# Order of work in a two-layer decoder trunk on 8 cores: row stores ahead of a routing chain, a weight load ahead of index scatters, norms one tile ahead, subtractions on another engine

## The chip, the cores and the metric

The kernel runs on all 8 cores of one Trainium2 chip. Each core takes one batch element of 2048 tokens and computes it alone; the cores exchange nothing. Cores 0 to 3 stand on one die, cores 4 to 7 on the other. The metric is the device time of the slowest core, in microseconds (us), lower is better.

The engines of a core are called PE (TensorE), DVE (VectorE), ACT (ScalarE), POOL (GpSimd) and SP (SyncE). Each runs its own instructions in program order and waits for the others by semaphores. SP, ACT and POOL issue DMAs.

## The reference

Two layers, and in each a token mixer, a hierarchical mixture of experts, and a gated embedding of the layer:

```
for i in range(2):
    xn = rms_norm(h, g_mix[i])
    mix = conformer_conv(xn) if i == 0 else moba_attention(xn)
    h = h + mix
    h = h + hier_moe(rms_norm(h, g_ffn[i]))        # group top-1, expert top-2 of 16
    h = h + sigmoid(rms_norm(h, g_ple[i]) @ w_gate) * (p[i] @ w_proj)

conformer_conv: u = xn @ w_pw1 + b; a, g = split(u); u = a * sigmoid(g)
                u = causal depthwise conv of width 31, over positions
                u = silu(layer_norm(u)) @ w_pw2 + b
hier_moe:       a group by softmax over 4, then 2 of its 4 experts, weights renormalised
                expert e: (silu(x @ w_gate[e]) * (x @ w_up[e])) @ w_down[e]
```

The model width is 1024, the expert hidden width 512, and a token goes to 2 of 16 experts.

## The kernel before

The residual stream h stays on chip, features on the partitions: 8 chunks of 128 features by 2048 tokens in float32. Tokens are worked in four tiles (tt 0 to 3) of 512. A small scheduler (`Sched`) puts a semaphore wait ahead of each instruction for every region that it reads or overwrites. The order of the instructions on each engine is the order in which the program's functions are called, so an engine that waits holds back all that was emitted behind it. DMAs of SP and ACT take their completion semaphores in turn from one pool, those of POOL from another (L60). A DMA waits for the last use of its semaphore.

The phases run in this order: A (convolution mixer), B0 (experts of layer 0), C0 (combination and embedding), D (attention), B1, C1.

**Phase A** (L578). At the start x is loaded in 16 DMAs, four for each tile. `rms_tile` (L557) makes a norm: ScalarE squares the eight chunks into two alternating buffers `sq`, TensorE sums them by a matmul with ones, ScalarE takes logarithm and exponential to give `rstd`, VectorE writes the normalised chunks `xgA`. `pw1(c, tt)` (L627) takes two groups of 8 matmuls, a sigmoid on ScalarE into one of two `sg` buffers chosen by tt, and a product on VectorE into `gp`. For each tile the norm and `pw1` of c = 0 and 1 are called; then `pw1` of the other chunks alternates with the convolution of chunk c - 2. `regroup` stores `gp` and reads it back in another layout. When the sums of the layer norm are complete, a loop over 32 groups (L695) subtracts the mean (`t1A`, on VectorE or POOL), multiplies by `rstd` (`t2A`, VectorE) and applies silu (ScalarE). After every four groups a store goes to memory and four loads bring it back as `xgA`, two of them issued by ScalarE, which waits for the store. `pw2(tt)` (L709) is the last matmul of the phase. It is not called there but handed to phase B as `tile_fn`. In layer 1 attention hands over its output projection in the same way.

**Front of phase B** (L954 to L1039), once for each layer. `front(tt)` (L833) squares and sums a tile and makes the router's logits, in turns between ScalarE and TensorE. `xnorm(tt)` writes the normalised tile `xnb`, `rows(tt)` (L824) transposes it into four blocks of 128 tokens, copies each on ScalarE into one of three `xrow` buffers, and stores it to memory in rows (`xnd`) by SP. `back(t0, nt)` (L850) is the routing chain of nt blocks of 128 tokens: some 90 small VectorE instructions, a prefix sum on TensorE (`Mall`), two products on POOL, and at its end two indirect DMAs per block from POOL, which scatter token numbers of 4 bytes into a list in memory (`idxd`). `wts` (L930) makes the combination weights: small VectorE instructions, one exponential on ScalarE, three POOL instructions that read `r_A`. `back` of the last four blocks writes `r_A` anew.

`load_w(e)` (L736) loads the weights of expert e into one of three ring buffers, in three DMAs. In layer 0 POOL issues them, with a cast from float32; in layer 1 SP issues them, from bfloat16 copies made during attention. The third ring buffer lies over memory of the mixer (its last weights and inputs), so `load_w(2)` waits for the last matmul of `tile_fn(3)`.

**The experts** then run one after the other: three gathers of 128 rows each from `xnd`, transposes, gate and up matmuls, silu and product, the down matmuls, and stores. Weights of expert e + 3 are loaded when expert e is done.

Of the kernel before, what the change touches and what calls it, by code (L numbers as in the profile page):

```python
# [18 lines left out]
NTT = 4  # L19
# [23 lines left out]
class Sched:  # L43
    def __init__(self, nc, ctx):
        self.nc = nc
        self.ctx = ctx
        self.eng = {'pe': nc.tensor, 'act': nc.scalar, 'dve': nc.vector, 'pool': nc.gpsimd, 'sp': nc.sync}
        self.sem = {}
        self.cnt = {}
        self.nsem = 0  # L50
        for e in ['pe', 'act', 'dve', 'pool']:
            self._new_sem(e)
        self.seen = {e: {} for e in self.eng}
        self.W = {}
        self.R = {}
        self.pend = {e: [] for e in self.eng}
        self.dma_sems = []
        self.dma_cnt = []
        self.dma_rr = {'hw': 0, 'sw': 0}
        self.dma_pool = {'hw': list(range(0, 8)), 'sw': list(range(8, 32))}  # L60
        for i in range(32):
            self.dma_sems.append(ctx.enter_context(nc.semaphore(f"dq{i}")))
            self.dma_cnt.append(0)
        self.nwaits = 0
        self.nops = 0
        self.addr = {}
        self.holes = [(SB0, SB1)]
        self.nm = 0
# [371 lines left out]
def build_program(phases=('A', 'B0', 'C0', 'D', 'B1', 'C1'), debug=False):  # L440
# [28 lines left out]
    with ExitStack() as ctx:  # L469
# [34 lines left out]
        def xn(c, lo, n):  # L504
            return xg[0][:, c, lo:lo + n]
# [51 lines left out]
        def rms_tile(tt, gname, gl, out_fn):  # L557
            ps = next_ps()
            for c in range(NC8):
                S.act(sq[:, c % 2, :], h[:, c, tts(tt)], AF.Square)  # L560
                S.mm(ps[:], ones_bf[:], sq[:, c % 2, :], start=(c == 0), stop=(c == NC8 - 1))
            S.act(rt[:], ps[:], AF.Ln, bias=EPS, scale=1.0 / D)
            S.act(rstd[:], rt[:], AF.Exp, scale=-0.5)
            for c in range(NC8):
                S.stt(out_fn(c), h[:, c, tts(tt)], P(gname, gl * 8 + c), rstd[:], ALU.mult, ALU.mult)
# [12 lines left out]
        def phase_A(pc):  # L578
# [3 lines left out]
            if True:  # L582
# [68 lines left out]
                def conv(c):  # L651
                    for gg in range(4):
# [7 lines left out]
                        if g:  # L660
                            stats(g - 1)

                for tt in range(NTT):
                    rms_tile(tt, 'g_mix', 0, lambda k, t1=tt: xn(k, t1 * TT, TT))
                    for c in range(2):
                        pw1(c, tt)
                S.copy('dve', blk[:], cva[:, NG * 36:NG * 36 + 128])
# [26 lines left out]
                ps_set[0] = list(range(8))  # L694
                for g in range(NG):  # L695
                    v = gc[:, g, 8:GW]
                    S.tt('dve' if g % 5 in (1, 3) else 'pool', t1[:, g % 3, :], v, mean[:], ALU.subtract)
                    S.tt('dve', t2[:, g % 3, :], t1[:, g % 3, :], rstd[:], ALU.mult)
                    S.act(v, t2[:, g % 3, :], AF.Silu, bias=P('ln_bP', g), scale=P('ln_gP', g))
                    c, gg = g // 4, g % 4  # L700
                    if gg == 3:
                        S.dma('sp', gpd[c], gc[:, 4 * c:4 * c + 4, 8:GW], outs=[("gpd", 0, 1, c, c + 1)])
                        for q in range(4):
                            S.dma('sp' if q % 2 else 'act', xg[0][32 * q:32 * q + 32, c, :].rearrange("p (i u) -> p i u", i=4),
                                  gpd[c].rearrange("(i c) g u -> g c i u", c=32)[q], ins=[("gpd", 0, 1, c, c + 1)])
# [14 lines left out]
        def phase_B(l, tile_fn, prev):  # L720
            EC = CO['ecol']
            with ExitStack() as pc:
# [97 lines left out]
                def xnorm(tt):  # L820
                    for c in range(NC8):
                        S.stt(xnb[:, tt % 2, c, :], h[:, c, tts(tt)], P('g_ffn', l * 8 + c), rstd[:], ALU.mult, ALU.mult)

                def rows(tt):  # L824
                    for i4 in range(4):
                        i = tt * 4 + i4
                        pb = next_ps()[:].bitcast(BF16)
                        for c in range(NC8):
                            S.transpose(pb[:, c * 128:(c + 1) * 128], xnb[:, tt % 2, c, i4 * 128:(i4 + 1) * 128], idb[:])
                        S.copy('act', xrow[:, i % 3, :], pb)  # L830
                        S.dma('sp', xnd[i * 128:(i + 1) * 128, :], xrow[:, i % 3, :], outs=[("xnd", 0, 1, i, i + 1)])
# [18 lines left out]
                def back(t0, nt):  # L850
# [71 lines left out]
                    S.tt('dve', ri[:], ri[:], ok2[:], ALU.mult)  # L922
                    S.ts('dve', ri[:], ri[:], dumpi[:], ALU.add, 0.0, ALU.max)
                    S.ts('dve', isl[:, T1], ri[:], float(NIDX - 1), ALU.min)
                    for i in range(t0, t0 + nt):
                        for k in range(2):
                            S.dma('pool', idxd, tokid[:, i:i + 1], out_idx=isl[:, i, k:k + 1],
                                  ins=[("idx", 0, 1, 50, 51)], outs=[("idx", 0, 1, 2 * i + k, 2 * i + k + 1)])
# [40 lines left out]
                front(2)  # L969
                rows(1)  # L970
                xnorm(2)
                back(0, 12)
                wts(0, 12)
                tile_fn(3)
                prev.close()
                ring.append(sb(f"ring_{l}_2", [128, 3 * NIN], BF16, pc))
                load_w(2)
                rows(2)
                front(3)
                back(12, 4)  # L980
                xnorm(3)
                rows(3)
                S.dma('sp', xi[:], idxd[0:IX1, :].rearrange("(p a) o -> p (a o)", p=128), ins=[("idx", 0, 1, 0, 51)])
# [761 lines left out]
```

How the kernel before makes its waits and increments, by code:

```python
    def _wait(self, engine, toks):  # L179
        need = {}
        for (sem, val, src) in toks:
            k = id(sem)
            if k not in need or need[k][1] < val:
                need[k] = (sem, val, src)
        for k, (sem, val, src) in need.items():
            if src == engine and engine == 'pe':
                continue
            if self.seen[engine].get(k, 0) < val:
                self.eng[engine].wait_ge(sem, val)
                self.seen[engine][k] = val
                self.nwaits += 1
# [19 lines left out]
    def op(self, engine, fn, ins=(), outs=(), inc=True):  # L211
# [6 lines left out]
                self._new_sem(engine)  # L218
            self.cnt[engine] += 1
            ins_obj.then_inc(self.sem[engine], 1)
            tok = (self.sem[engine], self.cnt[engine], engine)
# [907 lines left out]
        def overflow(l, nov_i, tok_nov, ovf, ring, xt, xT_, hdn, ysb, idb2, wfull, xs, c_loads, some):  # L1129
# [53 lines left out]
                for hc in range(4):  # L1183
                    A_.activation(out=sil[:, hc, :], in_=PS[hc][:, 0:n], func=AF.Silu)
                to(V)
                for hc in range(4):
                    V.tensor_tensor(out=hd[:, hc, :], in0=PS[4 + hc][:, 0:n], in1=sil[:, hc, :], op=ALU.mult)
            with nc.If(some > 0):
                for e in engs_:
                    for sem, cnt in state:
                        if cnt:
                            e.wait_ge(sem, cnt)
                nc.all_engine_barrier()
                nov, deep = val(1, NOV), val(2, 1)
                with nc.If(nov > NSP):
```

## Time and profile before

| | us |
|---|---|
| median of three runs | 2541.95 |
| lowest and highest | 2538.1 to 2543.45 |
| the profiled execution | 2535.46 |
| its span, core 5, the slowest | 2534.4 |
| its fastest core, core 1 | 2450.0 |

| engine of core 5 | busy us | share |
|---|---|---|
| PE matmul | 1796.5 | 71% |
| DVE | 941.1 | 37% |
| ACT | 836.5 | 33% |
| POOL | 462.2 | 18% |

The chain that ended last is PE for 48%, DMA 23%, DVE 10%, issue 7%, ACT 6%, another core or an unknown queue 4%. Times in all rows are us from the start of the core's span, and of core 5 if no other core is named. "Another core or an unknown queue" and "remote" stand for a release that the profile can't attribute. Names such as `ps<-xgA,w` are output and inputs of an instruction, `x32` is how many are merged in the row, and the bracket at a row's end says how long the engine was idle ahead of it and what ended that.

### The profile page before, as it was taken

What the parts mean: (1) busy time and instruction counts of PE and PEld (TensorE: products, weight loads), DVE (VectorE), ACT (ScalarE), POOL (GpSimd) and SP (SyncE); (2) the same over time, 40 slices, a digit from 0 to 9 for tenths busy, and PEclk for the clock granted to TensorE, in tenths of its full rate; (3) what the DMA queues carried; (4) which work ended last, traced back from release to release, by engine and by line L of the source; (5) the groups of instructions that cost most, each with busy time, mean ns of one, the idle gap of its engine ahead of it and who ended that gap; (6) DMA issues with size and microseconds to landing.
All of it is one profiled execution on the core that took longest, in us unless ns stands there. A gap on an engine that the chain in (4) does not pass through costs nothing.

```text
span 2534.4 us, 34160 instructions; the slowest of 8 cores (2450.0 to 2534.4 us)
## 1 busy us (share of the span) xinstructions
PE 1796.5 (71%) x11032; PEld 989.0 (39%) x11032; DVE 941.1 (37%) x1720; ACT 836.5 (33%) x1330; POOL 462.2 (18%) x522
## 2 busy tenths in 40 slices
PE   4799358329766666477777888787884269998587
PEld 1244122115333333233255666555622135554333
DVE  2566543332211111266533333333233223232265
ACT  2333413112111111156445555555421212222253
POOL 0000310422111111243200000000003121112354
PEclk8799678669887777678899999989987679999688
DMA  7153444148999999741276666696842059999862
GB/s 186 39 171 111 104 102 81 45 78 157 199 205 188 183 178 183 187 145 50 35 105 87 89 93 102 98 109 96 124 126 67 32 135 308 284 290 301 232 188 96
DMA packets 100593, 354.10 MB, mean 140 GB/s; under 512 B 13344, under 2 KB 25632, under 8 KB 81968
## 3 DMA queue, kind: packets, MB, share of 16 engines
q0 software_dynamic: 45472, 197.78, 45.5%
q1 hardware_dynamic: 52080, 150.79, 18.1%
q10 hardware_dynamic: 2848, 3.15, 0.5%
q8 instruction: 98, 1.61, 0.3%
q14 instruction: 95, 0.78, 0.1%
HBM read 393.61 MB, written 137.95 MB: 210 GB/s over the span
## 4 chain that ended last, share of the span: by engine, by line
PE 48%; DMA 23%; DVE 10%; issue 7%; ACT 6%; another core or an unknown queue 4%; POOL 1%; ACTq 0%; DVEq 0%; SPq 0%; POOLq 0%
PE ps L261 45%; DMA xt<-xnd,xi 12%; DMA ysd<-ysb 5%; PE ps L265 3%; DMA xt<-xnd,xs 2%; DMA gb<-ysd,slots 1%; ACT pt L278 1%; DMA gpd<-gc 1%; ACT sq L278 1%; DMA h<-xP 1%; DVE q L299 1%; DVE xgC L299 1%; DMA ring<-w 1%; DVE xnb L299 1%
## 5 line engine op out<-in xcount | busy, mean ns | idle before, releaser
L261 PE MATMUL ps<-xTT,ring 128*128 128x384 bf16 (+1 forms) x2304 | 367.6, 321 | 38.6 <-DVE ysb L305 22.9
L261 PEld LDWEIGHTS ps<-xTT,ring 128*128 128x128 bf16 x2304 | 218.2, 100 | 187.3 <-issue 58.1
L261 PE MATMUL ps<-xgA,w 128*128 128x512 bf16 x768 | 193.7, 408 | 86.4 <-DMA xgA<-gpd 69.0
L278 ACT ACTIVATE pt<-ps,cst_s 128x512 bf16<-128x512 f32 (+1 forms) x288 | 181.0, 658 | 83.2 <-PE ps L261 76.4
L261 PE MATMUL ps<-xgD,wh 128*128 128x512 bf16 x512 | 144.8, 434 | 85.7 <-DVE q L299 56.7
L265 PE MATMUL ps<-idb,xt 128*128 128x128 bf16 x800 | 72.2, 256 | 187.4 <-DMA xt<-xnd,xi 162.5
L261 PE MATMUL ps<-ring,hdn 128*128 128x512 bf16 x800 | 204.1, 416 | 0.3 <-DVE hdn L281 0.3
L261 PE MATMUL ps<-sq,ones_bf 128*128 128x512 bf16 x256 | 104.1, 443 | 113.5 <-ACT sq L278 110.2
L261 PE MATMUL ps<-xgC,ring 128*128 128x512 bf16 x512 | 144.0, 420 | 25.9 <-DVE h L281 14.3
L278 ACT ACTIVATE sq<-h 128x512 bf16<-128x512 f32 x192 | 111.0, 623 | 152.1 <-PE ps L261 124.7
L281 DVE TENSOR_TENSOR hdn<-ps,sgs 128x384 bf16<-128x384 f32 (+1 forms) x144 | 75.0, 527 | 229.8 <-PE ps L261 193.4
L261 PEld LDWEIGHTS ps<-xgA,w 128*128 128x128 bf16 x768 | 77.8, 102 | 200.4 <-issue 123.2
L304 ACT COPY ysb<-ps 128x512 f32<-128x512 f32 x100 | 57.9, 586 | 294.7 <-PE ps L261 198.5
L261 PE MATMUL ps<-qT,kT 128*128 128x256 bf16 x576 | 145.9, 278 | 0.5 <-ACT pt L278 0.4
L305 DVE COPY ysb<-ps 128x512 f32<-128x512 f32 x100 | 69.1, 692 | 199.6 <-PE ps L261 105.0
L261 PE MATMUL ps<-rh,esl 72*128 72x256 bf16 x576 | 142.9, 278 | 0.0
L265 PEld LDWEIGHTS ps<-idb,xt 128*128 128x128 bf16 x800 | 60.3, 115 | 201.3 <-issue 198.8
L244 POOL DMA_INDIRECT xt<-xnd,xi x96 | 92.9, 968 | 216.1 <-PE ps L265 187.4
L261 PEld LDWEIGHTS ps<-ring,hdn 128*128 128x128 bf16 x800 | 83.4, 106 | 105.1 <-issue 33.9
L278 ACT ACTIVATE sgs<-ps 128x384 f32<-128x384 f32 (+1 forms) x144 | 66.1, 468 | 175.3 <-PE ps L261 173.0
L305 DVE COPY xTT<-ps 128x1024 bf16<-128x1024 bf16 x68 | 46.9, 689 | 202.0 <-PE ps L265 172.8
L261 PE MATMUL ps<-vh,pt 128*128 128x129 bf16 x1088 | 113.6, 227 | 7.9 <-DVE pt L281 5.7
(209 smaller groups left out, 2631.1 us busy)
## 6 DMA issues: line engine op xcount, KB each, us to landing
ring<-w_moe POOLq DMA_DIRECT2D x48, 1024.0 KB
ysd<-ysb SPq DMA_DIRECT2D x96, 512.0 KB
w<-w_moe POOLq DMA_DIRECT2D x48, 1024.0 KB
ring<-w SPq DMA_DIRECT2D x48, 1024.0 KB
ysd<-zt SPq DMA_DIRECT2D x19, 512.0 KB
xnd<-xrow SPq DMA_DIRECT2D x32, 256.0 KB
yT<-h SPq DMA_DIRECT2D x32, 256.0 KB
h<-xP SPq DMA_DIRECT2D x14, 512.0 KB
```

What stands on the lines that cost most here:

```text
L244: ins_obj = self.eng[queue].indirect_dma_start(out, bass.IndirectOffsetOnAxis(out_idx, 0) if out_idx is not None else None, in_, bass.Indi ...
L261: return self.op('pe', lambda e: e.matmul(out, lhsT=lhsT, rhs=rhs, start=start, stop=stop, **kw), ins=[lhsT, rhs], outs=[out], inc=inc)
L265: return self.op('pe', lambda e: e.transpose(out, in_, ident), ins=[in_, ident], outs=[out])
L278: return self.op('act', lambda e: e.activation(out=out, in_=in_, func=func, **kw), ins=ins, outs=[out])
L281: return self.op(eng, lambda e: e.tensor_tensor(out=out, in0=in0, in1=in1, op=op), ins=[in0, in1], outs=[out])
L299: return self.op('dve', lambda e: e.scalar_tensor_tensor(out=out, in0=in0, scalar=scalar, in1=in1, op0=op0, op1=op1), ins=ins, outs=[out])
L304: return self.op('act', lambda e: e.copy(out=out, in_=in_), ins=[in_], outs=[out])
L305: return self.op(eng, lambda e: e.tensor_copy(out=out, in_=in_), ins=[in_], outs=[out])
```

## The change

It does these things:

- The semaphores for DMAs of SP and ACT become 12 instead of 8, those of POOL 20 instead of 24.
- In phase A the norm of tile tt + 1 is emitted ahead of `pw1` of tile tt.
- In the layer norm loop VectorE takes the subtraction of every fourth group (8 of 32) instead of two in five (13 of 32). POOL takes the rest.
- `rows(2)` is emitted ahead of `back(0, 12)` instead of behind `load_w(2)`.
- The scatters leave `back` for a function of their own. The first 24 are emitted behind `tile_fn(3)` and `load_w(2)`, and `wts(0, 12)` behind them. The last eight stay directly behind `back(12, 4)`.

```diff
-        self.dma_pool = {'hw': list(range(0, 8)), 'sw': list(range(8, 32))}
+        self.dma_pool = {'hw': list(range(0, 12)), 'sw': list(range(12, 32))}
...
+                def rms0(tt):
+                    rms_tile(tt, 'g_mix', 0, lambda k: xn(k, tt * TT, TT))
+
+                rms0(0)
                 for tt in range(NTT):
-                    rms_tile(tt, 'g_mix', 0, lambda k, t1=tt: xn(k, t1 * TT, TT))
+                    if tt + 1 < NTT:
+                        rms0(tt + 1)
                     for c in range(2):
                         pw1(c, tt)
...
-                    S.tt('dve' if g % 5 in (1, 3) else 'pool', t1[:, g % 3, :], v, mean[:], ALU.subtract)
+                    S.tt('dve' if g % 4 == 1 else 'pool', t1[:, g % 3, :], v, mean[:], ALU.subtract)
...
                     S.ts('dve', isl[:, T1], ri[:], float(NIDX - 1), ALU.min)
+
+                def scatter(t0, nt):
                     for i in range(t0, t0 + nt):
                         for k in range(2):
                             S.dma('pool', idxd, tokid[:, i:i + 1], out_idx=isl[:, i, k:k + 1],
...
                 xnorm(2)
+                rows(2)
                 back(0, 12)
-                wts(0, 12)
                 tile_fn(3)
                 prev.close()
                 ring.append(sb(f"ring_{l}_2", [128, 3 * NIN], BF16, pc))
                 load_w(2)
-                rows(2)
+                scatter(0, 12)
+                wts(0, 12)
                 front(3)
                 back(12, 4)
+                scatter(12, 4)
                 xnorm(3)
                 rows(3)
```

## Rows read from the trace of the kernel before

**Rows 1.** Medians of the two dies, from the view of the cores
```profile
die 0 (median of its cores): 2462.5 us, clock 0.845
die 1 (median of its cores): 2514.7 us, clock 0.841
```

**Rows 2.** The chain of waits, front of phase B0: start, us, what
```profile
476.52 16.33 another core or an unknown queue
```

**Rows 3.** Timelines of PE, ACT and DVE, first 125 us: start, us, instructions, idle before
```profile
29.15 12.09 PE L261 MATMUL ps<-xgA,w 128*128 128x512 bf16 x32 [2.49 <-DVE xgA L299]
77.03 12.04 PE L261 MATMUL ps<-xgA,w 128*128 128x512 bf16 x32 [3.69 <-DVE xgA L299]
85.70 1.28 ACT L278 ACT_TABLE_LOAD   x1 [9.67 <-PE ps L261]
91.72 5.46 PE L261 MATMUL ps<-sq,ones_bf 128*128 128x512 bf16 x8 [2.65 <-ACT sq L278]
99.98 5.39 DVE L299 SCALAR_TENSOR_TENSOR xgA<-h,prm_s,rstd 128x512 bf16<-128x512 f32 x8 [6.32 <-ACT rstd L278]
100.87 22.43 PE L261 MATMUL ps<-xgA,w 128*128 128x512 bf16 x80 [3.69 <-DVE xgA L299]
111.65 2.49 DVE L299 SCALAR_TENSOR_TENSOR gp<-ps,prm_s,sgA 128x512 bf16<-128x512 f32 x1 [6.29 <-PE ps L261]
```

**Rows 4.** Busy time by window, first 19 us; last: PEclk, DMA share, GB/s
```profile
0.00:19.00 19.00, 0.00 (x0) 0.00 (x0) 1.55 (x20) 0.00 (x0) 1.52 (x6) 1.00 0.87 189
```

**Rows 5.** Layer norm loop: chain (its first and last stores), timelines of POOL, DVE
```profile
286.42 3.19 DMA gpd<-gc
339.16 3.18 DMA gpd<-gc
315.36 1.51 POOL L281 TENSOR_TENSOR t1A<-gc,meanA 128x512 f32<-128x512 bf16 x1 [2.88 <-DVE t2A L281]
333.74 0.68 DVE L281 TENSOR_TENSOR t1A<-gc,meanA 128x512 f32<-128x512 bf16 x1
```

**Rows 6.** POOL's timeline, B0: first and last of 24 scatters, `wts`, last load
```profile
465.74 1.06 POOL L244 DMA_INDIRECT idxd<-tokid,r_isl  x1 [7.99 <-DVE r_d L281]
494.32 0.97 POOL L244 DMA_INDIRECT idxd<-tokid,r_isl  x1 [0.27 <-issue]
496.44 0.59 POOL L281 TENSOR_TENSOR wfull<-r_X,r_X 128x192 f32<-128x192 f32 x1
499.88 0.53 POOL L249 DMA_DIRECT2D ring<-w_moe  x1 [1.19 <-issue]
```

**Rows 7.** Timelines of PE and DVE, B0: `pw2(3)`, its updates, `r_A` of `back(12, 4)`
```profile
455.13 15.12 PE L261 MATMUL ps<-xgA,w 128*128 128x512 bf16 x64
466.79 8.38 DVE L299 SCALAR_TENSOR_TENSOR h<-ps,prm_s,h 128x512 f32<-128x512 f32 x8
523.86 0.47 DVE L281 TENSOR_TENSOR r_A<-r_oh,r_eq 128x64 f32<-128x64 f32 x2
```

**Rows 8.** ACT's timeline on core 0, B0: copies of `rows(2)`
```profile
468.38 2.84 ACT L304 COPY xrow<-ps 128x1024 bf16<-128x1024 bf16 x3 [5.93 <-PE ps L265]
```

**Rows 9.** Timelines of POOL, PE, ACT and DVE on core 5, front of B1
```profile
1933.86 1.08 POOL L244 DMA_INDIRECT idxd<-tokid,r_isl  x1 [8.79 <-DVE r_d L281]
1964.59 0.59 POOL L281 TENSOR_TENSOR wfull<-r_X,r_X 128x192 f32<-128x192 f32 x1
1942.44 0.26 PE L265 MATMUL ps<-idb,xnb 128*128 128x128 bf16 x1 [2.39 <-issue]
1969.13 1.01 ACT L304 COPY xrow<-ps 128x1024 bf16<-128x1024 bf16 x1 [35.37 <-remote]
1998.87 0.47 DVE L281 TENSOR_TENSOR r_A<-r_oh,r_eq 128x64 f32<-128x64 f32 x2
```

**Rows 10.** Busy time by window, B0, the third weight load; columns as above
```profile
500.00:520.00 20.00, 12.00 (x26) 1.98 (x26) 1.79 (x8) 8.19 (x13) 0.40 (x1) 0.76 0.98 179
```

**Rows 11.** The chain of waits in B0, the first gather behind weight loads
```profile
631.57 48.73 DMA xt<-xnd,xi
```

## The prediction

> **What bounds the kernel now.** I read the spans of the cores first. The time is that of the slowest core, core 5, and its whole die is slow: the medians of the dies stand 52.2 us apart [rows 1]. So an edit counts by what it does on that die. Second, the chain of waits of core 5, in order of time. From 348 us back it is a staircase in the first 125 us, a dense run of TensorE up to 273 us, and eight equal steps. In the front of the first mixture phase it holds a wait of 16.33 us for an unknown releaser, right behind a copy into `xrow` [rows 2]. Third, timelines of the single engines there, on core 5 and on core 0. The expert phase behind it is limited by transfers, and attention by TensorE; both start when the stage ahead ends, so a shift ahead of them is kept.
>
> **Part 1, norms one tile ahead.** Before, a tile costs TensorE 23.84 us (77.03 to 100.87): `pw1` starts, its first 16 matmuls end at 85.70, then a table load, a sigmoid, the 2.49 us product, a second sigmoid and a square follow, and the sums of squares start 6.02 us later, at 91.72; they take 5.46 us, and `pw1` of the next tile waits 3.69 us for logarithm, exponential and the first normalised slice [rows 3]. After, the sums of tile tt+1 stand ahead of `pw1` of tile tt, whose input is ready. The 3.69 us go, and so does the pacing of the first matmuls by the norm writes (5.39 us for eight slices). What is late next is VectorE: behind the end e of the sums, the norm writes of the next tile start at e+2.8 (97.18 to 99.98), end at e+8.2, and the first product stands behind them in VectorE's order, until e+10.7; sigmoid and square give e+12.2. By TensorE's own way (16 matmuls and 6.02 us) it is e+9.4 to e+12.8. I take 12.5, so a period is 18.0 us.
>
> Cost: `pw1` of tile 0 now waits for the squares of tile 1. They start behind tile 0's exponential, at about 28.9, and take 5.5: `pw1` starts at 34.4 instead of 29.15, 5.2 us later. Two periods bring it to 70.4. No sums come after that; tile 3's norm writes end at 78.6, and three products at 3.4 us each (2.49 and about 0.9 of hand-off) end the first product of tile 3 at about 88 at the latest. Before it ended at 111.65 + 2.49 = 114.1 [rows 3]. By VectorE that is 26 to 27 us; TensorE, with three pairs of banks in flight, reaches the convolution about 25 us earlier. **I take 25**, between 15 (a period of 21, with x tile 1 late by 4) and 28. Up to 273 us TensorE has no gap, so the gain stays.
>
> The twelve hardware semaphores hold four more x loads open at the start. In the first 19 us the queues moved 3.6 MB (189 GB/s), about tile 0 with the two parameter blocks (2.6 MB) and the two first weight loads (1 to 2 MB), and the squares start there, so the loads finish in order [rows 4]: I cost it at nothing, and at +16 at worst, when tiles 0 to 2 land together at 35 us. The twenty software ones cost nothing: the scatter that reuses one comes 25 us later.
>
> **Part 2, subtractions to POOL.** Thirteen of 32 are on VectorE, eight after. POOL takes 1.2 to 1.5 us for one, VectorE 0.68 alone. The loop is not set by either: its eight steps of 7.53 us (286.42 to 339.16 in seven) are four activations, a store that must land (3.2 us) and two issues on ScalarE's queue [rows 5]. POOL's 24 subtractions make 33 us of 60. Cost nothing; bounds -1 and +4. The Trainium skill ("GPSIMD Engine Reference", Performance versus the Vector engine) has elementwise work about twice as slow there. The trace agrees for one instruction (1.51 against 0.68 us); by that rule the five cost 5 x 0.8 = 4 us if they were on the path, and the chain shows them off it.
>
> **Part 3, the front of the mixture phases.** Before, on core 5, POOL issues 24 scatters of the lists from 465.74 to 495.3, then `wts`, then three weight loads until 500.4 [rows 6]. `pw2` of tile 3 runs on TensorE from 455.13 to 470.25 [rows 7]. The copies of `rows(2)` come behind it, in the scatters, and on this die they stand still until 493 and 501. Core 0 copies three of them from 468.38 without a gap [rows 8]. So `rows(2)` ahead of `back` takes the stall off the copies. Their transposes (32, 2 us) go into TensorE's wait for `Mall`.
>
> Does the stall go? In the second layer it is not in the copies alone: TensorE issues a transpose every 2.6 us while it waits for nothing (1942.44), and ScalarE gets the first eight transposes 31 us late, until 1969.13; the scatters there run from 1933.86 [rows 9]. On this die, TensorE's signals are late while scatters run, from some 5 us behind the first until 6 to 12 us behind the last. After the change `front(3)` stands in that window: 24 matmuls and eight squares in turns. It starts late too: `wts` is now behind `tile_fn(3)`, so ScalarE's exponential of `wts`, ahead of the squares, waits until VectorE has finished its eight updates of h and the sums, about 474.
>
> Layer 1. The scatters are where they were, since `load_w(2)` is on SP there. The squares start in the window (1944), one chunk per 3 signals gets through, and the rest follows when it closes at 1970 to 1975. The routing of tile 3 reaches `r_A` about 10 us before 1998.87. Bounds: 0 (nothing gets through), and 33.5, when nothing is late and `r_A` waits only for POOL's `wts`, which reads the old one (1964.59 + 0.6) [rows 9]. On core 0 a store behind the weight load goes from the path as well.
>
> Layer 0. Here POOL is passed by `load_w(2)`, which waits for TensorE's 470.25 and issues for 3.3 us. So the scatters begin at 473.9 instead of 465.74, 23 intervals of 1.24 us end them at 503.4, `wts` ends at 505.2, and `r_A` of `back(12, 4)` cannot come before 505.3: 18.6 us before its 523.86 [rows 6, 7]. On core 0 the same gate stood at about 494.5 and moves back by 8 us, but core 0 is not the slowest. The load itself gives nothing: expert 2 wants it after 600 us, and it was there by 520 [rows 10]. Under the window `front(3)` ends at about 505 and `r_A` is at 519, a gain of 5. **I take 5 and 10**, with bounds of -10 and 18.6 for layer 0, 0 and 33.5 for layer 1.
>
> A transfer behind weight loads on POOL's queue waits them out: the gather of an expert takes 48.73 us [rows 11]. The load held the engines for some 22 us [rows 10], so the scatters may land from 492 on, and the window then falls on `back(12, 4)`. The Trainium skill ("DMA: Bandwidth & Descriptors", Queues, rings and completion order) has each engine consume a queue's work in ring order; the gather's row agrees, and the fourth rival is what it gives at its worst.
>
> **Sum.** 25 + 0 + 10 + 5 = 40 us. The profiled execution took 2535.5 (span 2534.4); it goes to 2495. The median of the three runs is 6.5 above it, so 2541.95 - 40 = 2502; I say 2500.
>
> **Rivals.**
> 1. *The window moves with the work.* `front(3)` or `back(12, 4)` waits until it closes, as the copies did; both fronts give nothing, part 1 stays: 2517 (2512 to 2524). For it: in the second layer two engines are slow on TensorE's side, not the copies alone. Against: the copies' own 32 signals are out of the queue. 0.23.
> 2. *The stall was the copies'.* With their row stores gone from the scatters nothing is late: 25 + 18.6 + 33.5 = 77, 2465 (2460 to 2482). The slow die would then be near the other. Against: the 2.6 us spacing on TensorE. 0.20.
> 3. *The first stage gives less.* x tiles 0 to 2 land together and take 16 of the 25: 2518 (2512 to 2530). Against: the order of the loads above. 0.07.
> 4. *Slower.* The 24 scatters land behind the third weight load (492) and hold the window open. At 2.6 us each, the spacing seen on TensorE, it closes at 554, and `r_A` comes at about 568, 44 us later; with part 1 and layer 1 that is 44 - 25 - 10 = +9: 2551. It decides from 2.2 us per scatter on. Against: in layer 1 24 scatters and the window take 41 us together, 1.7 each. 0.05.
>
> **How the numbers follow.** Forecast 0.45, its own range 2486 to 2512. Within 0.2% (5 us, about what a measurement of this kernel tells from no change) no case has its centre: 0.02. Slower 0.05, faster 0.93. The range 2464 to 2524 leaves out the fourth rival, the end of the third, and some of the second.
>
> **What would show it.** Part 1: `pw1` pairs at about 34, 52, 70 and 81 us, the convolution from 103 instead of 128. Part 2: steps of 7.5 us as before. Part 3: the copies of `rows(2)` ahead of `Mall`; on core 5 waits of several us for TensorE inside `front(3)` or `back(12, 4)`; `r_A` at 494 and 1959 once the 25 us (and the 5) are taken off; core 0 later in layer 0 and 8 us earlier in layer 1. The forecast is wrong if the slow die shows no late signals, or if they last past `back(12, 4)`.

## The result and the profile after

The changed kernel takes 2467.5 us (median of 3 runs, 2459.43 to 2476.16) against 2541.95 before: ratio 0.9711, 95% interval 0.9655 to 0.9766, 74 us faster. The forecast was 2500 with a range of 2464 to 2524. Executions on record as slowed, most of them by a lower granted clock on all cores of a die, are left out of every median and ratio below; that leaves one to eight runs of each experiment. Each ratio is the one on record, with its 95% interval in brackets; it is not the quotient of the two medians that stand beside it, and differs from it by up to 0.006.

The spans of the cores after, from the view of the cores:

```profile
die 0 (median of its cores): 2448.3 us, clock 0.851
die 1 (median of its cores): 2423.4 us, clock 0.852
```

The gap between the dies was 52.2 us [rows 1] and is 24.9, and the slower die is now die 0. Its cores show in the second layer the late signals that core 5 showed before (waits of 5.7 to 7.4 us between the squares of `front(3)` on cores 0, 1 and 3, and of 7.1 us for the logarithm on core 2); the other die shows none in its fronts. In the first layer only core 3 is held for long; the logarithm waits 2.0 to 3.8 us on the other three. I call the die with the late signals the disturbed one. Which die it is does not belong to the kernel, and the slowest core of after (core 3) has to be read against the slowest of before (core 5).

TensorE in the first 100 us of core 3 (start, us, instructions, idle time before):

```profile
33.90 7.59 PE L261 MATMUL ps<-xgA,w 128*128 128x512 bf16 x32
44.91 5.46 PE L261 MATMUL ps<-sq,ones_bf 128*128 128x512 bf16 x8 [3.42 <-ACT sq L278]
50.17 7.98 PE L261 MATMUL ps<-xgA,w 128*128 128x512 bf16 x32
67.67 25.03 PE L261 MATMUL ps<-xgA,w 128*128 128x512 bf16 x112
98.34 1.89 PE L261 MATMUL ps<-gc,dg 128*128 128x512 bf16 x8
```

A pair of `pw1` runs in 7.6 us where the norm writes stretched it to 12.0 [rows 3], the periods (from one pair's start to the next) are 16.3 and 17.5 us, and the convolution starts at 98.3. VectorE between the first two pairs:

```profile
35.68 5.39 DVE L299 SCALAR_TENSOR_TENSOR xgA<-h,prm_s,rstd 128x512 bf16<-128x512 f32 x8 [2.14 <-ACT rstd L278]
40.99 2.48 DVE L299 SCALAR_TENSOR_TENSOR gp<-ps,prm_s,sgA 128x512 bf16<-128x512 f32 x1
```

The first product stands directly behind the eight norm writes, as forecast. The layer norm, from the chain of waits, still goes in steps of 7.52 us (308.21 less 255.58, in seven) [rows 5]:

```profile
255.58 3.30 DMA gpd<-gc
308.21 3.24 DMA gpd<-gc
```

The front of the first mixture phase on core 3. ScalarE, POOL, then VectorE:

```profile
416.73 2.84 ACT L304 COPY xrow<-ps 128x1024 bf16<-128x1024 bf16 x3 [0.77 <-PE ps L265]
443.58 1.91 ACT L278 ACTIVATE sq<-h 128x512 bf16<-128x512 f32 x3
455.76 0.63 ACT L278 ACTIVATE sq<-h 128x512 bf16<-128x512 f32 x1 [3.61 <-PE ps L261]
471.69 0.60 ACT L278 ACTIVATE rt<-ps 128x512 f32<-128x512 f32 x1 [15.31 <-remote]
...
441.99 1.04 POOL L244 DMA_INDIRECT idxd<-tokid,r_isl  x1 [0.27 <-issue]
470.55 0.96 POOL L244 DMA_INDIRECT idxd<-tokid,r_isl  x1 [0.27 <-issue]
...
483.88 0.47 DVE L281 TENSOR_TENSOR r_A<-r_oh,r_eq 128x64 f32<-128x64 f32 x2
```

The copies of `rows(2)` are done at 421, ahead of everything. The scatters run from 441.99 to 471.5 [rows 6]. ScalarE does its squares nearly unhindered and then waits 15.3 us with the logarithm; the view names no releaser on the core ("remote"). In the second layer, whose scatters start earlier against `front(3)`, the squares themselves are held:

```profile
1896.17 0.63 ACT L278 ACTIVATE sq<-h 128x512 bf16<-128x512 f32 x1 [0.66 <-issue]
1903.22 0.63 ACT L278 ACTIVATE sq<-h 128x512 bf16<-128x512 f32 x1 [6.42 <-remote]
1909.77 0.63 ACT L278 ACTIVATE sq<-h 128x512 bf16<-128x512 f32 x1 [5.92 <-remote]
1917.75 0.63 ACT L278 ACTIVATE sq<-h 128x512 bf16<-128x512 f32 x1 [7.35 <-issue]
1922.20 0.60 ACT L278 ACTIVATE rt<-ps 128x512 f32<-128x512 f32 x1 [3.83 <-remote]
```

One measure takes the shift ahead of a front out: **D**, the time from the `r_A` of the first three tiles to the `r_A` of tile 3, both on VectorE. Its landmarks, beside those of [rows 7], [rows 9] and the `r_A` of 483.88 above; first two of core 5 before, then three of core 3 after:

```profile
452.62 0.62 DVE L281 TENSOR_TENSOR r_A<-r_oh,r_eq 128x192 f32<-128x192 f32 x2
1919.81 0.62 DVE L281 TENSOR_TENSOR r_A<-r_oh,r_eq 128x192 f32<-128x192 f32 x2
422.21 0.62 DVE L281 TENSOR_TENSOR r_A<-r_oh,r_eq 128x192 f32<-128x192 f32 x2
1873.01 0.62 DVE L281 TENSOR_TENSOR r_A<-r_oh,r_eq 128x192 f32<-128x192 f32 x2
1931.07 0.47 DVE L281 TENSOR_TENSOR r_A<-r_oh,r_eq 128x64 f32<-128x64 f32 x2
```

With D the 76.0 us between the profiled spans (2534.4, 2458.4) split up:

| stretch (core 5 before, core 3 after) | forecast | measured |
|---|---|---|
| up to `r_A` of three tiles, layer 0 (452.62, 422.21) | 25 | 30.4 |
| D, layer 0 (71.2, 61.7) | 5 | 9.6 |
| from there to `r_A` of three tiles, layer 1 | 0 | 6.8 |
| D, layer 1 (79.1, 58.1) | 10 | 21.0 |
| behind it | 0 | 8.2 |

The forecast column holds what the prediction gave to each stretch. On the undisturbed die D went from 45.7 to 51.1 us in layer 0 and from 54.2 to 45.1 in layer 1 (core 0 before, core 4 after): later in the first layer and earlier in the second, as forecast for core 0.

### The profile page after: what moved, and what is told of

It reads as the page before. It is cut to its first block, busy times and chain, and to the rows that moved or that the text cites. A ratio compares the mean times of both kernels' runs of the same rounds, so it can differ in the third digit from the quotient of the medians.

```text
span 2458.4 us, 34207 instructions; the slowest of 8 cores (2412.2 to 2458.4 us)
## 1 busy us (share of the span) xinstructions
PE 1771.3 (72%) x11032; PEld 985.7 (40%) x11032; DVE 940.7 (38%) x1715; ACT 834.8 (34%) x1328; POOL 472.1 (19%) x527
## 3 DMA queue, kind: packets, MB, share of 16 engines
q0 software_dynamic: 45472, 197.78, 46.9%
## 4 chain that ended last, share of the span: by engine, by line
PE 52%; DMA 21%; DVE 10%; issue 7%; ACT 6%; another core or an unknown queue 3%; POOL 1%; ACTq 0%; DVEq 0%; SPq 0%; POOLq 0%
PE ps L261 48%; DMA xt<-xnd,xi 12%; DMA ysd<-ysb 4%; PE ps L265 3%; DMA xt<-xnd,xs 2%; ACT pt L278 1%; ACT sq L278 1%; DMA gpd<-gc 1%; DVE xnb L299 1%; DVE xgC L299 1%; DMA gb<-ysd,slots 1%; DVE q L299 1%; DMA h<-xP 1%; DVE gb L299 1%
## 5 line engine op out<-in xcount | busy, mean ns | idle before, releaser
L261 PE MATMUL ps<-xgA,w 128*128 128x512 bf16 x768 | 178.5, 394 | 70.3 <-DMA xgA<-gpd 68.1
L304 ACT COPY ysb<-ps 128x512 f32<-128x512 f32 x100 | 58.6, 586 | 280.8 <-PE ps L261 210.9
L305 DVE COPY xTT<-ps 128x1024 bf16<-128x1024 bf16 x68 | 46.9, 689 | 194.5 <-PE ps L265 173.7
```

The costliest lines, as they stand in the source:

```text
L261: return self.op('pe', lambda e: e.matmul(out, lhsT=lhsT, rhs=rhs, start=start, stop=stop, **kw), ins=[lhsT, rhs], outs=[out], inc=inc)
L304: return self.op('act', lambda e: e.copy(out=out, in_=in_), ins=[in_], outs=[out])
L305: return self.op(eng, lambda e: e.tensor_copy(out=out, in_=in_), ins=[in_], outs=[out])
```

## Experiments

Each was run in turns with the kernel before on one chip, in four groups on four chips: the first four, the next four, three, and the last. The first four are edits of the kernel before.

**Norms alone**, the first hunk of `pw1`'s loop:

```
+                rms0(0)
                 for tt in range(NTT):
-                    rms_tile(tt, 'g_mix', 0, lambda k, t1=tt: xn(k, t1 * TT, TT))
+                    if tt + 1 < NTT:
+                        rms0(tt + 1)
```

> Part 1 alone: the first norms one tile ahead, all else as before. My forecast priced it at 25 us. The trace after, where all parts are in, has the convolution start at 98.3 instead of 128.4 us on the slowest core and the projection behind it 30.9 us earlier. Theory A (the first stage's gain is kept to the end): 30 us faster than before, 26 to 33, and the start of the convolution at 98. Rival (part of it is lost where transfers set the end, in the expert phases): under 20 us faster, with the start of the convolution at 98 all the same.

Measured: 2489.8 against 2524.7, 34.9 us, a little over theory A's range; ratio 0.9865 (0.9821 to 0.991). The convolution starts at 98.67. All of part 1 reaches the end; the rival falls. D is as before, 72.0 and 72.3 us.

**The front alone**, the hunks of `scatter` and of the order of calls:

> Part 3 alone: row stores of the third tile ahead of back(0, 12), scatters behind the third weight load, wts behind the scatters; norms, subtractions and semaphores as before. My forecast: 15 us faster (5 in layer 0, 10 in layer 1). Theory A, from the trace after (9 us in layer 0, 26 to 34 in layer 1 on the slowest core): 35 to 45 us faster. Rival (what moved there is only which die the disturbance fell on, so the time saved is that of the undisturbed die): 15 to 25 us faster.

Measured: 2490.8, 33.9 us; ratio 0.9864 (0.982 to 0.9907), twice my 15 and just under theory A. The gain is the disturbed die's: its core 3 goes from 2523.6 to 2489.8 (medians), while on the other die three cores stay within 4 us and one is 12 us lower (2465.2, 2466.8, 2465.0 and 2455.7 before; 2453.3, 2463.2, 2465.9 and 2459.3). So the rival falls too: the gain is not the undisturbed die's. But D does not hold all of it. The profiled run was one of 2517 us, well above the median, and its D (66.6 and 64.9 us) is only 5 and 8 us under that of the run below; in the changed kernel it is some 10 and 15 under it. Even these leave 9 of the 33.9 us without a place.

**Subtractions and semaphores alone**, the two one-line edits:

> Subtractions of the layer norm (eight of 32 on VectorE instead of thirteen) and 12 hardware with 20 software semaphores alone. Both were priced at nothing: within 3 us of before, eight steps of 7.5 us in the layer norm. Rival (twelve hardware semaphores let more loads of x run at once at the start, to the cost of the first tile): up to 16 us slower, to be seen in the first sums of squares coming later than 21 us.

Measured: 2524.0 against 2524.7, ratio 1.0021 (0.9979 to 1.0062). The first sums of squares start at 20.5, the steps take 7.5 us. Costed right at nothing, the two together. D is 71.5 and 73.3.

**Row stores alone**:

```
                 xnorm(2)
+                rows(2)
                 back(0, 12)
                 wts(0, 12)
 ...
                 load_w(2)
-                rows(2)
```

> One step of part 3 alone: rows(2) ahead of back(0, 12); scatters, wts and third weight load stay where they are before. Theory A (the copies were what stood still for the late signals, and front(3) loses less to them): most of the gain of part 3, 20 to 35 us faster, and the scatters start at the old time, so layer 0 gains more than with the whole of part 3 (10 us and more on the slowest core). Rival (the move of the weight load ahead of the scatters is what gives the gain in layer 0): under 10 us faster, r_A of layer 0 where it was.

Measured: 2493.0 and 2500.6, so about 28 us; two runs give no interval. Core 3 took 2487.7 to 2500.7 us in all six executions, against a median of 2523.6 in the kernel before. D is 62.2 and 60.5 us, shorter by 10 and 12 than in the two kernels without the edit. One line carries most of part 3. Its ScalarE, while the scatters run from 463.13 to 492.7:

```profile
466.49 0.63 ACT L278 ACTIVATE sq<-h 128x512 bf16<-128x512 f32 x1 [0.44 <-DVE h L299]
473.58 0.63 ACT L278 ACTIVATE sq<-h 128x512 bf16<-128x512 f32 x1 [6.46 <-remote]
480.87 0.63 ACT L278 ACTIVATE sq<-h 128x512 bf16<-128x512 f32 x1 [6.67 <-remote]
488.88 0.63 ACT L278 ACTIVATE sq<-h 128x512 bf16<-128x512 f32 x1 [7.38 <-issue]
497.62 0.63 ACT L278 ACTIVATE sq<-h 128x512 bf16<-128x512 f32 x1 [8.11 <-remote]
```

One chunk per 7.1 to 8.7 us, and a chunk is three matmuls in the trace: the "one chunk per 3 signals" of the forecast. Three is the number of TensorE's instructions, though, not surely that of its signals: the program calls two matmuls per chunk (L838 and L839), each with one signal, and the float32 one of the router stands in the trace as two (`ps<-h,wrg`, x2). In the kernel before, TensorE started its transposes 2.6 us apart in the same place [rows 9], which is nearly the same rate for each instruction. The next four are the changed kernel and three edits of it, and ask whether the number of signals is what counts.

**The changed kernel again**:

> The changed kernel itself, as the yardstick of this group. If the parts add up (34 us for the norms and 34 for the front, each measured alone), it is 65 to 75 us faster than before. Rival (the parts overlap): under 60.

Measured: 2472.9 against 2525.5, 52.7 us; ratio 0.9757 (0.9698 to 0.9816), from three runs. By the medians that is the rival's size; by the ratio it is 61 us. The product of the two parts' ratios, 0.9731, lies inside the interval, and the first measurement gave 74. The runs don't decide between the two. D of core 3 is 68.4 and 58.7 us: in layer 0 this execution gained 3 us on the kernel with its front unchanged (71.5), where the one above gained 10.

**Fewer signals of TensorE**:

```
-            ins_obj.then_inc(self.sem[engine], 1)
+            if engine != 'pe' or Sched.KEEP is None or (self.pesem, self.cnt['pe']) in Sched.KEEP:
+                ins_obj.then_inc(self.sem[engine], 1)
```

The program is built twice; `KEEP` is filled in the first pass with the signals that somebody waits for.

> The changed kernel with fewer signals of TensorE: only those of its instructions on whose completion somebody waits count up its semaphore, 1792 instead of one for every instruction; every wait stays at the same instruction. In the front of rows-only the squares ran at one per 7.3 us in the scatters, which is three signals of 2.4 us. Theory S (the late signals stand in a line and each takes some 2.4 us, the time of two scatters): with one signal per square instead of three or four the squares run without a stall of over 3 us, the disturbed die comes near the other, and the kernel gains 15 to 30 us on the changed one. Rival B (a signal is late whatever their number, since the engine's semaphore write waits for the scatters themselves): squares and the logarithm wait as before and the time is that of the changed kernel, within 5 us.

Measured: 2465.7, ratio 0.9821 (0.9761 to 0.988), from three runs. Against its yardstick nothing, though with such intervals (0.006 is 15 us) the time alone could hide the 15 us that theory S asked for at least; the waits can't. In layer 1 the squares wait 7.7, 5.9 and 8.1 us as before, D is 58.6. Theory S falls.

**Scatters back at their old place**:

```
                 back(0, 12)
+                scatter(0, 12)
+                wts(0, 12)
                 tile_fn(3)
 ...
                 load_w(2)
-                scatter(0, 12)
-                wts(0, 12)
```

> The changed kernel with scatters and wts back at their old place, ahead of the projection of the fourth tile and of the third weight load; row stores, norms, subtractions and semaphores as in the change. In the kernel with the row stores alone the undisturbed die was about 15 us earlier than with the whole front, the disturbed one 5 us later. Theory A: the same here, so the slowest core is 3 to 8 us later than in the changed kernel and the median of the undisturbed die 10 to 20 us earlier. Rival (the two orders are the same to the slowest core, since the window of late signals is as long in both): within 3 us of the changed kernel.

Measured: 2469.3, ratio 0.9793 (0.974 to 0.9847), the same as the changed kernel within the intervals; the cores of the undisturbed die are at 2418 to 2426, in the changed kernel at 2422 to 2427. D on the undisturbed core 7 is 9 us shorter in layer 0 (43.4, 52.5) and equal in layer 1; the end shows none of it. The rival holds: no effect of moving the scatters behind the third load can be seen.

**Both**:

> Both: scatters at their old place and fewer signals of TensorE. Theory S: the scatters run beside the projection of the fourth tile, end 8 to 10 us earlier than in the change, and nothing waits for late signals, so this is the fastest of the four: 20 to 40 us under the changed kernel. Rival B: as the kernel with the scatters back, nothing from the signals.

Measured: 2468.2, ratio 0.976 (0.9699 to 0.982): again nothing from the signals. But with one signal per chunk (only the sum of squares is waited for) its trace shows how late a single one is. `sq` has two slots, so a square waits for the matmul two chunks back. TensorE and ScalarE of core 3:

```profile
444.27 0.38 PE L283 MATMUL ps<-sq,ones_bf 128*128 128x512 bf16 x1
444.58 1.03 PE L283 MATMUL ps<-h,wrg 128*20 128x512 f32 x2
450.10 0.58 PE L283 MATMUL ps<-sq,ones_bf 128*128 128x512 bf16 x1 [4.49 <-ACT sq L300]
...
449.33 0.63 ACT L300 ACTIVATE sq<-h 128x512 bf16<-128x512 f32 x1 [5.20 <-remote]
455.88 0.63 ACT L300 ACTIVATE sq<-h 128x512 bf16<-128x512 f32 x1 [5.92 <-remote]
463.89 0.63 ACT L300 ACTIVATE sq<-h 128x512 bf16<-128x512 f32 x1 [7.38 <-remote]
```

The matmul that ended at 444.65 is heard of at 455.88, 11.2 us later; that of 450.68 at 463.89, 13.2 later. The other way is prompt: the square that ends at 449.96 lets a matmul start at 450.10. Every signal is late by itself, with two under way. That gave theory L (a fixed latency, in the text before the run with eight slots). The Trainium skill ("Perfetto Trace Analysis", Per-engine timelines) has the end of a matmul in the profile as an estimate, with the signal pushed once the results are written and then spread to all engines, a tail that the profile does not show. The trace agrees in kind: the matmuls last 0.4 to 0.6 us as ever, and the 11 to 13 us lie behind their ends, where no row of TensorE has them. The page gives no length for the tail.

**No scatters of the first three tiles**. The kernel leaves them out, so their list entries stay zero and the gathers read row 0. It ran once. Its 2553.5 us say nothing of the change, since the stretch between the fronts and the one behind them are each some 60 us or more longer; only the fronts count:

> The changed kernel without the 24 scatters of the first three tiles (they are left out, so the lists of those tiles stay at zero and the experts gather row 0; only the fronts of the mixture phases are read). Theory L (the signals of TensorE reach ScalarE and VectorE late on one die because of these scatters): no wait of over 3 us for a signal in front(3) on any core in either layer, and r_A of tile 3 comes at about 458 in the first layer on all cores, where the changed kernel has it at 484 to 490 on the slowest core. Rival (the lateness comes from row stores or the weight load, which stand at the same place): waits of 6 to 19 us in front(3) on one die as before.

```profile
448.96 0.63 ACT L278 ACTIVATE sq<-h 128x512 bf16<-128x512 f32 x1 [0.66 <-PE ps L261]
450.25 0.63 ACT L278 ACTIVATE sq<-h 128x512 bf16<-128x512 f32 x1 [0.66 <-PE ps L261]
452.83 0.60 ACT L278 ACTIVATE rt<-ps 128x512 f32<-128x512 f32 x1 [1.95 <-PE ps L261]
```

No late signal in `front(3)` on any core, in either layer. The one that is left is at the copy of the counts, in the eight scatters of tile 3: on core 3 it waits 8.4 us (layer 0) and 9.6 (layer 1), on core 7 3.9 and 3.7. D is 40.0 to 41.5 us on all eight cores in layer 0 and 38.3 to 39.0 in layer 1, so the two dies are alike there; `r_A` of layer 0 comes at 461.2 and 466.5 (I had said 458). The scatters are the cause, and row stores and weight load, which are still there, are not. The whole price of the scatters on core 5 was 71.2 - 40.0 = 31 us in layer 0 and 79.1 - 38.9 = 40 in layer 1; the change took back 9.6 and 21.0 of it. Core 5 was a costly one: core 3, with its front unchanged (the run of the subtractions and semaphores), has 71.5 - 40.0 = 31 and 73.3 - 38.9 = 34, of which the change takes back 10 and 15. And not all of the price is late signals. Between the same two kernels the undisturbed die, which has none, goes from 45.7 to 46.9 us down to 40.1 to 41.5, and from 50.9 to 56.6 down to 38.3 to 39.0.

**Eight slots for the squares of tile 3**, on top of the scatters at their old place:

```
-                        S.act(sq[:, c % 2, :], h[:, c, tts(tt)], AF.Square)
+                        s = xnb[:, 1, c, :] if tt == 3 else sq[:, c % 2, :]
+                        S.act(s, h[:, c, tts(tt)], AF.Square)
 ...                                # the sum of squares reads s too
```

> The changed kernel with the scatters at their old place (as in the run of that order) and one more edit: the eight squares of tile 3 go into eight slots of their own instead of two in turn, so that ScalarE waits for no signal of TensorE between them. With fewer signals the squares stood still as before, and each signal read alone was 11 to 14 us late with two under way. Theory L (each signal is late by a latency, and many can be under way): the squares run without a gap, only the logarithm waits once, 10 to 15 us, and one more late signal follows at the transposed logits; r_A of layer 0 on the disturbed die 5 to 12 us earlier, that of layer 1 10 to 20 earlier. Rival W (signals are held until the window closes): the logarithm then waits until the scatters end, and r_A stands where it was, within 3 us.

Measured: 2466.6, ratio 0.9799 (0.9758 to 0.984), no gain. ScalarE and POOL of core 3:

```profile
446.35 0.63 ACT L278 ACTIVATE xnb<-h 128x512 bf16<-128x512 f32 x1 [0.42 <-issue]
450.17 0.63 ACT L278 ACTIVATE xnb<-h 128x512 bf16<-128x512 f32 x1 [3.19 <-issue]
473.31 0.60 ACT L278 ACTIVATE rt<-ps 128x512 f32<-128x512 f32 x1 [22.52 <-remote]
...
466.30 0.96 POOL L244 DMA_INDIRECT idxd<-tokid,r_isl  x1 [0.27 <-issue]
```

The squares run through and the logarithm waits 22.5 us (28.8 in layer 1), until 6.0 us behind the end of the last scatter (5.9 in layer 1). The last of the 24 matmuls ends at 453.56 (1905.41), so its signal is 19.7 us late (21.5). D goes from 58.9 to 57.3 and from 64.6 to 58.4. A fixed latency of 13 us would have freed the logarithm at about 467: theory L falls. Holding everything until the window closes fits here, but not the chunks that got through inside it in the runs above. What fits both is a rate: some 7 us for three matmuls, signalled or not, so that 24 at once don't get through in time. A delay that grows through the window would fit both too; no run tells them apart.

**Products of `wts` on VectorE and the counts ahead**, with the eight slots (the product for tile 3's expert numbers and the sum `wfull` go to VectorE too):

```
-                        S.tt('pool', (X2 if k else X3)[:], A[:]...
+                        S.tt('dve', (X2 if k else X3)[:], A[:]...
 ...
                 back(12, 4)
+                (the 16 matmuls of the counts and their copy n16)
                 scatter(12, 4)
```

> The run with the eight slots, and two things more: the products of wts and the expert numbers of tile 3 on VectorE instead of POOL, so that nothing of tile 3's routing stands behind POOL's scatters; and the counts per expert (sum of Mall and its copy) ahead of the scatters of tile 3, where their signal was 8 us late. Theory: on the undisturbed die r_A comes 5 to 10 us earlier in both layers (its gate was POOL), on the disturbed die 8 us per layer go behind the scatters of tile 3; in all 15 to 35 us under the changed kernel, about 2440. Rival (what the fronts gain is given back where the first gather waits for its list): within 5 us of the run with the eight slots.

Measured: 2465.8 against 2523.4, ratio 0.9767 (0.9744 to 0.979). On the undisturbed die it does what was expected: D 37.4 and 36.8 on core 7, the cores at 2405 to 2412, some 15 us ahead of the changed kernel. The disturbed die still waits for the window (D 57.3 and 58.3), and the slowest core is where it was. The expectation, about 2440, misses by 25 us.

**The window kept from `front(3)`**, with the eight slots and the products on VectorE:

```
                 back(0, 12)
+                scatter(0, 4)
+                wts(0, 12)
                 tile_fn(3)
 ...
                 load_w(2)
-                scatter(0, 12)
-                wts(0, 12)
-                front(3)
+                S.wait_tok('pool', front(3))
+                scatter(4, 8)
+                msum(0, 12)              # one reduce of Mall over tiles, bf16
                 back(12, 4)              # its ranks: 5 matmuls, not 16
+                msum(1, 16)
+                (one matmul for the counts and the copy n16)
                 scatter(12, 4)
```

> Built on what the runs showed: without the scatters the routing of tile 3 takes 40 us from the r_A of the first three tiles to its own, in their window 59 to 65; squares get through at one per 7 us whether their matmuls carry one signal or three; and with eight slots the logarithm, behind 24 matmuls, waits until 6 us after the last scatter. So the window is kept from front(3): eight scatters go at once behind back(0, 12), the other sixteen wait on POOL for the end of front(3); in their window TensorE gets 5 small matmuls for the ranks instead of 16 and one for the counts instead of 16 (the sums over tiles are made on VectorE). Products of wts on VectorE and eight slots for the squares as before. Theory Q (TensorE's instructions report one by one, one per 2.4 us, while scatters are under way, so the number of its instructions decides): r_A of tile 3 comes 40 us behind the first r_A in both layers, the copy of the ranks is late by at most 12 us, the first gather of layer 0 is issued at 500 to 508 instead of 521 to 529 on the slowest core, and the kernel is 20 to 45 us faster than the changed one. Rival W (nothing of TensorE is reported before the window closes): the copy of the ranks waits until 6 us behind the sixteen scatters, the first gather comes at 513 or later, and the kernel is within 12 us of the one with the counts ahead.

Measured: 2432.3 against 2536.0, ratio 0.9618 (0.955 to 0.9687): the fastest of all, 104 us under the kernel before. On this chip die 1 is the disturbed one, in the kernel before as well. D is 37.9 on core 3 and on core 7 in layer 0, and 38.0 in layer 1; the first gather of layer 0 is issued at 501.6 on the slowest core, in the changed kernel at 521.0 and 529.0 (two executions). The two dies are 16.5 us apart. What D gained on the run before (57.3 and 58.3 there) comes from the split of the scatters, since the sums over tiles feed only what stands behind `r_A`; what each of the two gave to the time wasn't measured alone. It did not run beside the changed kernel: 0.9618 stands against its 0.9711 and 0.9757, and only with the first of these do the intervals overlap, by 0.003.

As a test of the rate it says nothing, since the copy of the ranks slipped in before the window opened. VectorE of core 7, whose sixteen scatters start at 454.88:

```profile
459.63 0.41 DVE L281 TENSOR_TENSOR r_A<-r_oh,r_eq 128x64 f32<-128x64 f32 x2
461.00 0.22 DVE L305 COPY r_tmp<-ps 128x64 f32<-128x64 f32 x1 [0.62 <-PE ps L261]
...
464.82 0.24 DVE L281 TENSOR_TENSOR r_sf<-r_sf,r_ov 128x8 f32<-128x8 f32 x1
466.16 0.17 DVE L281 TENSOR_TENSOR r_sf<-r_sf,r_ok 128x8 f32<-128x8 f32 x1 [1.09 <-DVE r_sf L281]
...
472.74 0.17 DVE L281 TENSOR_TENSOR r_s<-r_s,r_ov 128x8 f32<-128x8 f32 x1 [3.20 <-issue]
...
474.92 0.17 DVE L299 SCALAR_TENSOR_TENSOR r_ri<-r_s,r_ri 128x8 f32<-128x8 f32 x1 [1.70 <-remote]
...
480.95 0.17 DVE L290 TENSOR_SCALAR r_isl<-r_ri 128x8 int32<-128x8 f32 x1
```

From 465 on, 10 us after the first of these scatters, VectorE's steps that need its own result wait 0.5 to 3.2 us where they follow each other at 0.3 us before and after; `r_A` to `r_isl` takes 21.3 us, on core 3 of the same run 10.6. So the lateness is not TensorE's alone.

## Why the prediction was right

The direction and the parts were right; the size was forecast at little more than half. 2467.5 lies outside the 2486 to 2512 that the forecast gave itself, and 3.5 us inside the wider range, in the part that was held open for the second rival. That it lies in there at all is in part luck, as follows.

*Part 1.* The mechanism and its steps stand: VectorE sets the period, and the gain is kept to the end. The term was sized too small: 30.4 us (34.9 alone) for 25. In the first period the norm writes come 1.6 us behind the sums and the next sums 10.8 behind (sums to 34.1, then 35.68 and 44.91), where I had 2.8 and 12.5: both rest on rows of a later tile, where ScalarE loads a table (1.28 us) ahead of the logarithm. In the second period they are 2.8 and 12.0. So the two periods take 33.8 us instead of 36.0. The rest of `pw1` up to the convolution takes 30.7 instead of 32.6, and its start, 33.9, was forecast at 34.4: the convolution begins at 98.3 instead of 103. (The first product of tile 3 is at 88.8 by the forecast's own terms, not 88.)

*Part 2 and the semaphores.* Nothing, as costed.

*Part 3.* The late signals persist and `r_A` moves forward all the same; in the second layer the squares crawl through them at one chunk per three matmuls, as forecast. Both terms were too small by one step, the way from the end of the wait to `r_A`. I had `front(3)` end at 505 and `r_A` at 519, 14 us. Without scatters `r_lb`, the last result of `front(3)`, comes at 455.57 and `r_A` at 461.16, 5.6 us, and from the start of the logarithm 8.3. In layer 0 that error was partly hidden by a second: I let `front(3)` end 1.6 us behind the last scatter (503.4), though I had written that signals are late until 6 to 12 us behind it. It ended 6.8 behind (471.5, `r_lb` at 478.29). Set back by the 30.4 us, the scatters ended 1.5 us earlier than forecast, the wait 5.2 later behind them, and `r_A` came 8.4 sooner behind the wait: 5 + 1.5 - 5.2 + 8.4 makes 9.7, and 9.6 was measured. Nor did the squares stand in the window there, as I had it; only the logarithm did. In layer 1 I let the window close 50 to 55 us behind the first `r_A` and put `r_A` 69 us behind it [rows 9]. The logarithm came 49 us behind the first `r_A` (1922.20 - 1873.01), and `r_A` 8.9 later: 21 us instead of 10, of which about 6 belong to core 5, whose D of 79.1 was above the 72.3 and 73.3 of core 3 in two kernels with the same front.

*Rivals.* The first, nothing from the fronts, is refuted by the front alone (33.9 us). The second, nothing late once the copies are gone, by every trace of a changed kernel; yet its time, 2465, is the nearest to 2467.5, because the terms above were small. It would have been the right number for a wrong reason. The third falls with the norms alone (34.9 us) and the semaphores' null result. The fourth needs the scatters to hold the window open behind the third load; they end at 471.5 with `r_A` at 483.9, and no effect of the order of load and scatters can be seen.

*What stays open.* 15 us of the 76 lie in stretches with the same instructions, between the fronts and behind them. The 8.2 us at the end are most likely not the change's: core 3 takes 527.0 us there in the run of the subtractions and semaphores, whose expert phases are as before, and 527.3 after; core 5 before took 535.5. The middle stretch takes 1388 to 1402 us on core 3 in the changed kernel and the experiments (the one without scatters apart), without a pattern I could name. Core 3 against core 3, that run and the changed kernel, the 66.7 us between the spans (2525.1, 2458.4) are 29.5, 9.8, 12.6, 15.2 and -0.3 in the order of the table. Also open is what the rate counts. Fewer instructions of TensorE inside the window, with everything else in place, would tell; that was not tried.

A third thing is open, and the kept traces point at it. They hold a record of every update of a semaphore, and on the disturbed die a part of these records is missing in every profile: before, 23640 to 23899 on cores 4 to 7 against 26111 to 26149 on cores 0 to 3; after, 23703 to 24026 on cores 0 to 3 against 26134 to 26155; in the last experiment it is die 1 again. That fits the view's "remote", which says that no release was found. Even without the 24 scatters, the cores of die 0 have over 1000 records fewer than those of die 1, and its fronts show no late signal. Whether the recording itself takes part in the delay was not tested. An execution timed without it would tell.

## What to carry to other kernels

When the cores of one die wait for something that the profile puts down to no engine, look for what POOL issues at that time before blaming the engine that waits. Measure such a stretch from a landmark in front of it, on both dies, and run once without the suspected transfers: that gives the whole price, here 31 and 40 us on core 5 (31 and 34 on core 3), before any reordering is paid for. Compare the same core on the same die where a run has it. Cures that leave the chain inside the window (fewer signals, more slots) left its waits as they were; the kernel that keeps the chain out of it is the fastest. And a chain's tail behind a wait is read from a place where nothing disturbs it, not from the disturbed one.

## What the runs showed of the hardware

- While 24 scatters of 4-byte elements are issued at one per 1.24 us, signals between engines are late on one of the two dies: 11 to 13 us for a single one of TensorE's, 19.7 and 21.5 us for the last of 24 matmuls sent at once. It begins some 7 to 10 us after the first scatter. The wait that was held at the end of the scatters ends 5.7 to 6.2 us after the last one (eight waits: the kernel before on cores 5 and 7, eight slots and products on VectorE on core 3); on core 5 before, a later copy waited until 11.9 us after. ScalarE's signals to TensorE were prompt; VectorE's to itself were late too.
- Eight scatters are enough: the copy of the counts, behind 16 matmuls in the scatters of tile 3, waits 7.7 to 8.4 us on each core of the disturbed die after, in both layers, and 3.7 to 3.9 on each core of the other. In the last experiment the eight that run ahead of `front(3)` hold nothing up: on core 7 they end at 444.7, and the logarithm, at 450.85, waits 2.1 us.
- The die is the chip's or the run's: die 1 in the profile before, die 0 after and in the three groups of experiments behind it, die 1 in the last. Within a group it stayed the same one in the kernel before.
- The disturbed die is the one whose trace lacks semaphore records (23640 to 24026 of some 26100 per core, before and after).
